# Opening stage of a fused decoder step: the norm weight as one row, the order of the first loads, and the first two weight pieces swapped

## The reference

```
h = x * rsqrt(mean(x*x) + 1e-6) * g_mix          # RMSNorm of 1056 rows of 1024
z = h @ w_in                                     # (1056 x 1024) @ (1024 x 6996)
q_g, k_g, v_g, r_g, a_low, q_d, k_d, v_d, q_i, k_i, w_i, gate_g, gate_d = split(z)
k_i = layernorm(k_i)                             # indexer keys, 64 wide
score = sum_h relu(q_i[h] . k_i) * w_i[h]        # 4 indexer heads; top-k keys per query
# then sparse attention over the chosen keys, gated linear attention (its gate from a_low),
# two branch projections, output projection, RMSNorm, SwiGLU FFN, final RMSNorm
```

## Time and profile before

| | us |
|---|---|
| median of 3 runs | 2027.96 |
| lowest and highest run | 2027.02, 2030.35 |
| the profiled execution's own time | 2030.28 |
| its span in the profile | 2028.6 |
| TensorE busy | 1976.8 (97% of the span) |
| VectorE, ScalarE, GpSimd busy | 1033.6, 632.7, 312.4 |

### The profile page before, as it was taken

One profiled execution on the slowest core, in us unless ns is written; L12 is line 12 of the kernel. 1 busy time (PEld: TensorE's weight loads), 2 busy tenths in 40 slices (PEclk: granted clock), 3 DMA queues, 4 the chain that ended last, 5 costly groups with the idle time before them and its releaser, 6 DMA issues.

```text
span 2028.6 us, 31188 instructions
## 1 busy us (share of the span) xinstructions
PE 1976.8 (97%) x12165; PEld 1806.5 (89%) x12165; DVE 1033.6 (51%) x2228; ACT 632.7 (31%) x1130; POOL 312.4 (15%) x327
## 2 busy tenths in 40 slices
PE   6899999999999999999999999999999999999997
PEld 6599999999999888888799978999899889988995
DVE  5699995344454423666754336424432443344335
ACT  5533212223333364555543224111111121121113
POOL 3343223232222241001033200000000000000000
PEclk9999999999999999999999999999999999999998
DMA  5132332222221263444654311101110110111002
GB/s 165 37 90 85 117 109 92 75 85 73 71 66 57 70 194 113 152 167 156 241 173 134 103 67 63 63 1 63 63 59 4 63 63 23 41 63 63 1 32 86
DMA packets 144100, 174.44 MB, mean 86 GB/s; under 512 B 9561, under 2 KB 120959, under 8 KB 143455
## 3 DMA queue, kind: packets, MB, share of 16 engines
q1 hardware_dynamic: 136638, 148.89, 22.0%
q0 software_dynamic: 7328, 23.67, 3.4%
HBM read 127.83 MB, written 44.40 MB: 85 GB/s over the span
## 4 chain that ended last, share of the span: by engine, by line
PE 92%; DVE 3%; ACT 2%; issue 1%; DMA 1%; SPq 0%; POOL 0%; DVEq 0%; ACTq 0%; POOLq 0%
PE ring L941 26%; PE ring L943 26%; PE ring L942 25%; PE ring L1101 3%; PE ring L936 3%; PE lgt L1091 2%; PE ring L1261 1%; PE ring L1268 1%; PE ring L1264 1%; PE lgt L1339 1%; PE ring L1047 1%; DVE arena L2470 0%; DVE arena L1992 0%; PE ring L1232 0%; DVE arena L2446 0%
## 5 line engine op out<-in xcount | busy, mean ns | idle before, releaser
L941 PE MATMUL ring<-n_hi,piece_hi 128*128 128x352 f32 (+1 forms) x1312 | 435.3, 332 | 2.6 <-ACT arena L1409 1.9
L943 PE MATMUL ring<-n_hi,piece_lo 128*128 128x352 f32 (+1 forms) x1312 | 423.5, 323 | 0.0
L942 PE MATMUL ring<-n_lo,piece_hi 128*128 128x352 f32 (+1 forms) x1312 | 422.9, 322 | 0.0
L1409 ACT ACTIVATE arena<-ring 128x352 f32<-128x352 f32 (+7 forms) x367 | 152.9, 439 | 407.4 <-PE ring L943 294.0
L941 PEld LDWEIGHTS ring<-n_hi,piece_hi 128*128 128x128 f32 (+1 forms) x1312 | 247.0, 188 | 10.8 <-issue 6.9
L942 PEld LDWEIGHTS ring<-n_lo,piece_hi 128*128 128x128 f32 (+1 forms) x1312 | 247.6, 189 | 0.5
L943 PEld LDWEIGHTS ring<-n_hi,piece_lo 128*128 128x128 f32 (+1 forms) x1312 | 246.7, 188 | 0.4
L2006 DVE TENSOR_SCALAR_CACHE_REDUCE arena<-arena 128x384 uint8<-128x384 f32 (+6 forms) x224 | 190.6, 874 | 1.4 <-DVE arena L2006 0.2
L2531 POOL TENSOR_TENSOR piece_lo<-piece_whole,piece_hi 128x1024 fp32r<-128x1024 f32 (+2 forms) x48 | 109.4, 2279 | 502.8 <-ACT piece_hi L1422 502.6
L941 PE MATMUL ring<-h_hi,gate_hi 128*128 128x352 f32 x528 | 170.6, 323 | 0.7 <-DVE act_whole L2484 0.7
L941 PE MATMUL ring<-h_hi,up_hi 128*128 128x352 f32 x528 | 170.3, 322 | 0.0
(11 more groups left out here) (310 smaller groups left out, 3626.8 us busy)
## 6 DMA issues: line engine op xcount, KB each, us to landing
piece_whole<-w_in SPq DMA_DIRECT2D x54, 512.0 KB, 3.6
projected_rows<-arena SPq DMA_DIRECT2D x44, 528.0 KB, 2.7
arena<-projected_rows SPq DMA_DIRECT2D x12, 1056.0 KB, 6.6
gate_whole<-w_ffn_gate SPq DMA_DIRECT2D x11, 1024.0 KB, 7.0
up_whole<-w_ffn_up SPq DMA_DIRECT2D x11, 1024.0 KB, 5.1
down_whole<-w_ffn_down SPq DMA_DIRECT2D x11, 1024.0 KB, 4.9
arena<-projected_rows SPq DMA_DIRECT2D x16, 528.0 KB, 3.6
arena<-x_prompt SPq DMA_DIRECT2D x16, 512.0 KB, 6.8
```

What stands on the lines that cost most here:

```text
L941: pe.matmul(out, lhi, rhi, start=first, stop=False)
L942: pe.matmul(out, lhi, rlo, start=False, stop=False)
L943: return pe.matmul(out, llo, rhi, start=False, stop=last)
L1409: evacuates(act.activation(dst, src, ACT.Copy, scale=scale), *key)
```

## The change

It does the following. (1) The norm weight comes as one row of 4 KB on one partition; TensorE multiplies a row of ones with it in two matmuls of 512 columns into a PSUM tile (`gain`, the second of the two wide tiles, not of the ring), and VectorE reads it from there in the product. (2) The SP queue issues the weight row, x tiles 0 and 1, the identity, tile 2, the page table, tile 3, piece 0, tile 4, piece 1, tiles 5 to 8, and only then the small rows, whose transposes run just ahead of kiT. (3) Piece 0 is now a full piece of indexer queries, piece 1 the mixed one, in two DMAs since its columns are ordered otherwise; TensorE's list of blocks becomes (0,0), (1,0), (1,1), (0,1), the pages, (1,2), mt, (0,2), (2,2), (2,0), and as vec leaves the front, the ring's indices of the opening fall by one. (4) The lists of ScalarE, VectorE and GpSimd are reordered: the root of tile 0 ahead of the square of tile 1, `norm_hi(4)` ahead of `square_x(7)` and `first_out(0, 0)`, the high half of piece 1 behind that of tile 3, `norm_input` ahead of the next `mean_tile`, the table of the relative bias behind the input tiles, the first low half behind 5 index pages. Lines that only rename rows or columns, and the semaphores' declarations, are left out.

```diff
@@ -192,9 +192,9 @@
         def piece_of(kind, f, parts, k=KD):
             pieces.append((kind, f, parts, k))
-        piece_of("mi", 0, [("w_in", COL["ki"], IDM, 0), ("w_in", COL["al"], RANK, IDM), ("w_in", COL["wi"], IH, IDM + RANK)])
-        for f in range(2):
-            piece_of("qi", f, [("w_in", COL["qi"] + P * f, P, 0)])
+        piece_of("qi", 0, [("w_in", COL["qi"], P, 0)])
+        piece_of("mi", 0, [("w_in", COL["al"], RANK, 0), ("w_in", COL["ki"], IDM + IH, RANK)])
+        piece_of("qi", 1, [("w_in", COL["qi"] + P, P, 0)])
         for k in ("kd", "vd", "qd"):
             for f in range(4):
                 piece_of(k, f, [("w_in", COL[k] + P * f, P, 0)])
@@ -259,7 +259,7 @@
         def early_groups(i):
-            return {3: [(0, 0)], 5: [(1, 0)], 6: [(0, 1)], 8: [(1, 1), (0, 2)]}.get(i, [])
+            return {3: [(0, 0)], 5: [(1, 0)], 6: [(1, 1)], 8: [(0, 1), (1, 2)]}.get(i, [])
         def nb_after(n, g):
             return range(4 * g, 4 * g + 4) if n == 3 and g < 2 else []
@@ -293,19 +293,19 @@
         def plan_d(n, g):
             plan("d", n, g)
-        plan("vec")
         for i in range(NT):
             plan("h", i, 0), plan("h", i, 1)
             for k in early_groups(i):
                 plan_d(*k)
-                if k == (1, 1):
+                if k == (0, 1):
                     for n in range(4):
                         plan("ps", n)
         for c in range(2):
             plan("mt", c)
-        plan_d(1, 2)
+        plan_d(0, 2)
         plan_d(2, 2)
         plan_d(2, 0)
+        plan("vec")
         for n in range(3):
             plan("kiT", n)
         for n, k in enumerate(SCC):
@@ -440,8 +440,8 @@
...
-        alT = mT[IDM:IDM + RANK, :]
-        al_hi, al_lo = halves("al_hi", o_sg, T)[IDM:IDM + RANK, :], halves("al_lo", o_sg + T, T)[IDM:IDM + RANK, :]
+        alT = mT[0:RANK, :]
+        al_hi, al_lo = halves("al_hi", o_sg, T)[0:RANK, :], halves("al_lo", o_sg + T, T)[0:RANK, :]
@@ -459,6 +459,8 @@
...
+        ones_row = arena[0:1, B_vd + 2560:B_vd + 2560 + P]
+        gain = lgt[1]
@@ -693,7 +694,7 @@
...
-        N_FIRST, N_REST = 5, 6
+        N_REST = 11
@@ -745,23 +746,23 @@
             def load_x(i):
                 sp.dma_start(xa[i][0:rows(i), :], x_src(i)).then_inc(x_landed[i], 16)
+            sp.dma_start(grow[0:1, :], a["g_mix"]).then_inc(grow_in, 16)
+            load_x(0)
+            load_x(1)
             sp.dma_start(arena[:, o_c128:o_c128 + P], a["c128"][:, 0:P]).then_inc(c_first, 16)
-            load_x(0)
-            sp.dma_start(grow, a["g_mix"].to_broadcast([P, D])).then_inc(grow_in, 16)
-            sp.dma_start(vrow[0:8, :], a["g_mix"].rearrange("l (k p) -> (l k) p", p=P)).then_inc(c_first, 16)
-            sp.dma_start(vrow[8:16, :], a["g_ffn"].rearrange("l (k p) -> (l k) p", p=P)).then_inc(c_first, 16)
-            sp.dma_start(vrow[16:20, :], a["b_gate"].rearrange("l (k p) -> (l k) p", p=P)).then_inc(c_first, 16)
-            sp.dma_start(vrow[20:22, :], a["gla_norm_g"].rearrange("l (k p) -> (l k) p", p=P)).then_inc(c_first, 16)
-            sp.dma_start(relb[0:NB, :], a["rel_bias"]).then_inc(relb_in, 16)
-            load_x(1)
+            load_x(2)
             sp.dma_start(pagetab[0:1, :], a["page_table"].rearrange("(o b) g -> o (b g)", o=1)).then_inc(pagetab_in, 16)
-            load_x(2)
+            load_x(3)
             load(0)
-            load_x(3)
             load_x(4)
             load(1)
             for i in range(5, NT):
                 load_x(i)
+            sp.dma_start(vrow[0:8, :], a["g_mix"].rearrange("l (k p) -> (l k) p", p=P)).then_inc(c_rest, 16)
+            sp.dma_start(vrow[8:16, :], a["g_ffn"].rearrange("l (k p) -> (l k) p", p=P)).then_inc(c_rest, 16)
+            sp.dma_start(vrow[16:20, :], a["b_gate"].rearrange("l (k p) -> (l k) p", p=P)).then_inc(c_rest, 16)
+            sp.dma_start(vrow[20:22, :], a["gla_norm_g"].rearrange("l (k p) -> (l k) p", p=P)).then_inc(c_rest, 16)
+            sp.dma_start(relb[0:NB, :], a["rel_bias"]).then_inc(c_rest, 16)
             sp.dma_start(arena[:, o_c128 + P:o_c128 + n128], a["c128"][:, P:n128]).then_inc(c_rest, 16)
             sp.dma_start(arena[0:32, o_c32:o_c32 + n32], a["c32"]).then_inc(c_rest, 16)
             sp.dma_start(bits, a["cbits"]).then_inc(c_rest, 16)
@@ -999,39 +1000,44 @@
                                     start=g == 0, stop=g == 1)
                 done(ins, "ss")
-            pe.wait_ge(c_first, 16 * N_FIRST)
-            transposes(("vec",), [(0, vrow[0:22, :])])
+            pe.wait_ge(one_set, 1)
+            pe.wait_ge(grow_in, 16)
+            for c in range(2):
+                pe.matmul(gain[:, 512 * c:512 * c + 512], ones_row, grow[0:1, 512 * c:512 * c + 512],
+                          start=True, stop=True).then_inc(gain_full, 1)
+            pe.wait_ge(c_first, 16)
             for i in range(NT):
                 pe.wait_ge(x_h, i + 1)
                 for c in range(2):
                     transposes(("h", i, c), [(P * s, xa[i][0:rows(i), (4 * c + s) * P:(4 * c + s + 1) * P])
                                              for s in range(4)])
                 for n, g in early_groups(i):
-                    if n == 0:
+                    if (n, g) in ((0, 0), (1, 1), (1, 2)):
                         for k in range((3 * g), min(NT, 3 * g + 3)):
                             for c in range(2):
                                 wait_evac(pe, "h", k, c)
                     dense(n, g)
-                    if (n, g) == (1, 1):
+                    if (n, g) == (0, 1):
                         pe.wait_ge(pg_landed, 16 * DB * NPG)
                         for k in range(4):
                             transposes(("ps", k), [(P * s, kpg[:, 4 * k + s, :]) for s in range(4)])
             for g in range(3):
-                wait_evac(pe, "d", 0, g)
+                wait_evac(pe, "d", 1, g)
             for c, (i0, i1) in enumerate(MT_TILES):
                 transposes(("mt", c), [(MI * (i - i0), mT[0:MI, i * P:i * P + rows(i)]) for i in range(i0, i1)])
-            dense(1, 2)
+            dense(0, 2)
             dense(2, 2)
             dense(2, 0)
             pe.wait_ge(c_rest, 16 * N_REST)
+            transposes(("vec",), [(0, vrow[0:22, :])])
             pe.wait_ge(kn_done, 1)
             for n in range(3):
                 transposes(("kiT", n), [(P * s, kn[0:rows(4 * n + s), 4 * n + s, :])
                                         for s in range(4 if n < 2 else 1)])
             for n in range(3):
                 wait_evac(pe, "kiT", n)
-                wait_evac(pe, "d", 1, n)
+                wait_evac(pe, "d", 0, n)
             for n, (b, h, c0, w_) in enumerate(SCC):
                 if score_groups(n):
                     dense_part(2, 1, score_groups(n)[0], score_groups(n)[-1] + 1)
@@ -1442,7 +1448,7 @@
...
-                dst = mT[0:MI, t0:t0 + tn] if n == 0 else qiT[:, n - 1, t0:t0 + tn]
+                dst = mT[0:MI, t0:t0 + tn] if n == 1 else qiT[:, n // 2, t0:t0 + tn]
@@ -1461,10 +1467,8 @@
             act.wait_ge(one_set, 1)
             link(act.activation(ort[:, 0:1], one, ACT.Sqrt))
             square_x(0)
+            root_x(0)
             square_x(1)
-            root_x(0)
-            act.wait_ge(c_first, 16 * N_FIRST)
-            copy_out(vec, bank("vec")[:, 0:22], "vec")
             square_x(2)
             root_x(1)
             norm_hi(0)
@@ -1475,15 +1479,15 @@
             square_x(4)
             root_x(3)
             norm_hi(2)
-            hi_piece(1)
             square_x(5)
             root_x(4)
             norm_hi(3)
+            hi_piece(1)
             square_x(6)
             root_x(5)
+            norm_hi(4)
             square_x(7)
             first_out(0, 0)
-            norm_hi(4)
             root_x(6)
             norm_hi(5)
             square_x(8)
@@ -1491,25 +1495,26 @@
             first_out(1, 0)
             norm_hi(6)
             root_x(8)
-            first_out(0, 1)
+            first_out(1, 1)
             norm_hi(7)
             norm_hi(8)
-            first_out(1, 1)
+            first_out(0, 1)
             for n in range(4):
                 copy_out(kiS[:, 2 * n:2 * n + 2, :], bank("ps", n).rearrange("p (a b) -> p a b", a=2), "ps", n)
-            first_out(0, 2)
+            first_out(1, 2)
             hi_piece(2)
             act.wait_ge(zeroed, 1)
             copy_out(kw[:, 0:5, :], bank("mt", 0)[:, 0:5 * MI].rearrange("p (a b) -> p a b", a=5), "mt", 0)
             wait_full(act, "mt", 1)
             act.activation(kw[:, 5:8, :], bank("mt", 1)[:, 0:3 * MI].rearrange("p (a b) -> p a b", a=3), ACT.Copy)
             copy_out(kw[0:NS, NTP, :], bank("mt", 1)[0:NS, 3 * MI:4 * MI], "mt", 1)
-            first_out(1, 2)
+            first_out(0, 2)
             hi_piece(3)
             act.wait_ge(kv_done, 1)
             act.activation(krt, kvar, ACT.Sqrt).then_inc(krt_done, 1)
             first_out(2, 2)
             first_out(2, 0)
```

(35 more changed lines are left out.)

3 lines of the change are left out of this document (1 added, 2 removed).

## The result

The change made the kernel a little slower, by less than the 0.2% that the prediction takes as what a measurement tells. Over 22 runs of each the median went from 2027.32 to 2030.81 us; the ratio is 1.0014, with a 95% interval of 1.0008 to 1.0020. The forecast was +4.2 us; the medians are 3.5 us apart and the ratio makes it 2.8 us (1.6 to 4.1 by its interval).

A forecast was written before the change was run, and what follows sets the result against it. TensorE, 92% of the span, was taken as the bound. The terms -3.7 + 1.6 + 4.4 + 0.2 + 1.7 gave +4.2 us, from a median of 2027.96 to 2032.2 us, range 2028.2 to 2036.0.

The forecast's parts named there:

- The bound: Whole kernel: TensorE is 92% of the span, and a shift of TensorE in the opening is carried to the end.
- first rival: Clock: no fall behind piece 2's wait, or clock up before the first block; +2.3, 2030.3 us, chance 0.30.
- The opening, -3.7: Before the first dense block: fewer loads ahead and earlier products start it at 18.7 instead of 22.43.
- The gain at nothing: Opening: two TensorE matmuls of the weight row, 0.98 us each, ready near 6.1 when VectorE wants the gain; no cost.
- The clock in the first block: First dense block: length kept at 5.92 us; a clock up before it would take 2.1 off, as a bound.
- The ring, +1.6: Between the first two dense blocks: tile 5's last transposes wait for ScalarE's later copy out; 3.8 us instead of 2.17.
- The slot, +4.4: Ahead of block (2,2): piece 2 shares piece 0's slot, so its halves wait for (0,2); TensorE stands 4.4 us.
- The vector copy, +0.2: Ahead of the scores: the moved vector transposes' copy stands among ScalarE's copies the scores wait for; bound 0 to 0.3.
- the fall, +1.7: Block (2,2): one clock fall to 1.2 GHz behind the 4.4 us wait costs 1.7 us; other end 0.
- The second (two falls): Between the first two blocks: the 3.8 us stretch of only transposes brings another fall; +1.7, 2033.9 us, chance 0.22.
- The third: Opening gives less, with tiles or gain 1 to 1.5 us late; +5.4, 2033.4 us, chance 0.13.
- fourth: Block (2,2): the shared slot causes no wait; sum -1.9, 2026.1 us, chance 0.05.

The follow-up runs named there:

- the run meant for it: Kernel with mixed piece and copy out first, given the earlier load order and amount, including a broadcast to 127 partitions: 2044.59 us, first block at 39.75.
- the one that waits 2.0: Changed kernel with the copy out first, three of four subtractions for piece 2's low half left out; wait of 2.0 us, no run time given.
- the slots' edit: Changed kernel with piece 2 taking the slot of piece 1, and piece 3 that of piece 0: 2025.62 against 2027.83 us, ratio 0.9985.
- the first four experiments: Changed kernel with slots in the other turn (0.9985), copy out first (1.0012), both (0.9975), or old piece order with copy out first (0.9973).
- the small rows alone: Kernel with mixed piece and copy out first, piece ahead of tile 3, identity and five small rows loaded early, no broadcast: first block 19.29, scores 61.77.
- the experiment on the weight: Changed kernel with slots in the other turn and copy out first, norm weight again a 512 KB DMA broadcast: first block 20.32, scores 62.82.

## Why the prediction was right, and where it was off

**The bound.** Right: TensorE's start of the scores moved by 3.5 us, and the medians of the runs by as much (the ratio says 2.8). The prediction gave 0.50 to a loss that a measurement tells and 0.45 to none; with a ratio of 1.0014 it was the second. By the ratio the result lies nearer to the first rival (+2.3) than to the forecast (+4.2), by the medians and the scores nearer to the forecast.

**The opening, -3.7.** It was -3.24. Two landings were taken too early: tile 0 came at 4.78 and not 4.5, and tile 2 only at 8.51, so that ScalarE waited for it 0.95 us with the root of tile 1 behind it; so the products ended at 8.0, 11.3, 13.9 and 17.5 against 7.65, 10.3, 13.1 and 16.65. What made the 3.2 us was shown only in part. The product of tile 3 did take 1.28 us instead of 2.50, but it took 1.28 with the weight in SBUF too, where GpSimd paid instead; so that PSUM alone made this gain isn't shown. The broadcast costs 1.1 us at the block and the small rows 0.6 where each was put back; that these sum up to the whole was not shown, as the run meant for it failed. Of the two things that the prediction named as holding the tiles back, the late root of tile 0 is worth nothing at the block once tile 1 lands early. Tile 3's late landing did hold the products of tiles 2 and 3 before, but that the mixed piece's issue made it late has no support: with the piece (in two loads) ahead of tile 3 again the block came no later. The size was near, the reason for it partly another.

**The gain at nothing.** Right by two errors. The matmuls took 3.75 us and not 1.96: transposes were the wrong row to take for an fp32 product, and so the term was put at nothing with half of the true cost in it. The page of the Trainium skill that the prediction weighed against them (FP8 and Floating Point Precision, "TensorE Precision Notes", four passes) gave 3.4 (an estimate from the page), and the trace with its 3.75 sides with the page. The 1.4 us that the prediction worked out from it is the delay of the gain; the product, which starts at 6.35 in its sum, would have been some 1.1 late. But the row landed at 2.42 and not 3.9, and so the gain stood at 6.2, ahead of the product at 6.74.

**The clock in the first block.** Left at 5.92 in the sum, with 2.1 less as a bound; it was 4.85, and between 4.5 and 5.6 in the other kernels with this opening. This is the largest error of the sum, 1.07 us.

**The ring, +1.6.** 1.40 measured, and the whole of it went when the copy out was put first.

**The slot, +4.4.** 4.31 by the starts, 4.09 as a wait; the line that frees the slot removed it. VectorE's key normalisation made no wait of its own, as assumed: it ended at 64.5 and TensorE arrived at 67.09.

**The vector copy, +0.2, and the fall, +1.7.** 0.26 and 1.76. The fall is tied to the wait by the profiles: it is there in both that wait 4.1 us, and gone in the one that waits 2.0 and in those that don't wait there.

**Rivals.** The second (two falls) did not happen: the stretch of 3.57 us between the first two blocks, with only transposes in it, brought none, in this profile or in that of the slots' edit, which has the same stretch; so that the stretch would look idle throughout, as the rival supposed, was not borne out. The first came half true, by the earlier rise within the first block. The third and fourth were ruled out by the start of the block and by the wait.

## What to carry to other kernels

Before swapping the order in which buffers are consumed, look for what is tied to their numbers: here the slot of the halves went by parity, and a change of the first two pieces made the third wait for work that had moved behind it; a place in an in-order list ahead of which a copy out frees a bank is such a tie too. Two hidden waits of this kind (1.4 and 4.3 us, with a clock fall of 1.8 behind the second) outweighed a first block that ended 4.3 us earlier, 3.2 by its start and 1.1 by the clock. Where a stage's gain is a few us of 2000, compare the start of the next stage in the profiles, as runs scatter by more.

## What the runs showed beyond that

- The time of a whole run goes with its mean granted clock. Over the 22 runs of the changed kernel the span and the mean granted clock go together (correlation -0.95, fitted by least squares): 1.3 us for each 0.001 of mean clock, from 2026.0 us at 0.996 to 2031.7 at 0.992. The profiled execution had the clock at 0.996, with one fall ahead of the last 20 us (near 58 us), that of the kernel before 0.994 with four (near 91, 738, 768 and 986); so it came out shorter with a later start of the scores. Falls were counted in profiles only; that their number makes the scatter of the other runs is an inference from the mean clock. For the kernel before the tie is looser (35 runs beside the first four experiments: -0.71, 1.1 us for each 0.001).
- The time for which a DMA issue holds its queue isn't the cost of that DMA: 4.27 us at the mixed piece in the earlier trace rows, 1.01 us for nearly the same loads with fewer bytes issued ahead of them, and then 3.87 for two plain tiles.
- Behind a broadcast to 127 partitions the whole core moved 25 to 30 GB/s, the next issue held the queue for 9.62 us and tile 1 was squared only at 28.13 (at 7.57 with the small rows alone); the one to 128 partitions, issued behind tile 0 in the experiment on the weight, cost 1.1 us at the first block.
